# Expert weights in eighteen places instead of sixteen, token rows kept once in fp32 and gathered by fp32 products

## The reference

```python
def expert_choice_ffn(h, w_router, w_gate, w_up, w_down):   # h: 512 tokens x 1024
    cap = CAPACITY_FACTOR * seq // N_EXPERTS                 # 64 tokens for each of 16 experts
    aff = softmax(h @ w_router)
    gate, idx = lax.top_k(aff.transpose(0, 2, 1), cap)       # each expert chooses its tokens
    xe = h[idx]                                              # gather: 16 x 64 rows
    a = silu(xe @ w_gate) * (xe @ w_up)                      # 1024 x 1024 each
    ye = (a @ w_down) * gate
    y = zeros.at[idx].add(ye)                                # scatter
```

## Time and profile before

| | us |
|---|---|
| median of 3 runs | 1550.1 (1548.37 to 1550.99) |
| span of the profiled execution | 1550.0 |
| PE busy | 1457.8 (94%) |
| PEld busy | 955.4 (62%) |
| DVE busy | 615.2 (40%) |
| ACT busy | 492.6 (32%) |
| POOL busy | 74.5 (5%) |
| L809, the expert weights' products, busy | 351.1 |
| chain that ended last: PE | 76% |
| chain that ended last: DMA | 11% |
| of it DMA of `w_up`, `w_gate`, `w_down` | 5%, 4%, 2% |
| HBM read | 303.35 MB |

### The profile page before, as it was taken

How to read it: one execution, slowest core, us unless ns; L and a number is a source line. 1 busy time by engine, 2 the same in 40 slices (tenths; PEclk the granted TensorE clock), 3 DMA queues, 4 the chain that set the end, 5 groups by cost and what they waited for, 6 DMA issues and landing times.

```text
span 1550.0 us, 17611 instructions
## 1 busy us (share of the span) xinstructions
PE 1457.8 (94%) x7135; PEld 955.4 (62%) x7135; DVE 615.2 (40%) x1192; ACT 492.6 (32%) x912; POOL 74.5 (5%) x100
## 2 busy tenths in 40 slices
PE   8988988999999999999997999988898999999998
PEld 6855366455434433433323899966686888888886
DVE  5366666344122222222215532136675443154325
ACT  6355276331001101101104412367734333123321
POOL 2000000100000000000002200000001111001100
PEclk9999999998999999999998999999999999999999
DMA  7476350318999999999995131140011332233201
GB/s 231 81 291 266 127 246 1 149 62 343 421 421 421 421 422 420 422 421 421 421 421 210 42 108 56 56 163 1 31 65 55 109 109 88 76 109 109 105 32 55
DMA packets 82738, 310.27 MB, mean 200 GB/s; under 512 B 7188, under 2 KB 43309, under 8 KB 55906
## 3 DMA queue, kind: packets, MB, share of 16 engines
q1 hardware_dynamic: 80656, 305.34, 50.3%
q10 hardware_dynamic: 1202, 2.15, 1.2%
q0 software_dynamic: 800, 1.66, 0.4%
HBM read 303.35 MB, written 5.78 MB: 199 GB/s over the span
## 4 chain that ended last, share of the span: by engine, by line
PE 76%; DMA 11%; ACT 5%; DVE 5%; issue 1%; SPq 0%; DVEq 0%; ACTq 0%
PE ps L809 15%; PE ps L433 13%; PE ps L434 13%; PE ps L435 13%; DMA sb<-in_w_up 5%; PE ps L663 4%; DMA sb<-in_w_gate 4%; DMA sb<-in_w_down 2%; PE ps L760 1%; PE ps L530 1%; ACT sb L1072 1%; PE ps L936 1%; PE ps L797 1%; PE ps L574 1%; PE ps L620 1%
## 5 line engine op out<-in xcount | busy, mean ns | idle before, releaser
L809 PE MATMUL ps<-sb 128*64 128x512 f32 x1536 | 351.1, 598 | 12.6 <-DMA sb<-in_w_gate 4.3
L809 PEld LDWEIGHTS ps<-sb 128*64 128x64 f32 x1536 | 103.3, 136 | 217.4 <-issue 181.9
L1072 ACT ACTIVATE sb<-ps 128x512 f32<-128x512 f32 (+4 forms) x168 | 86.2, 528 | 251.0 <-PE ps L785 73.1
L434 PE MATMUL ps<-r_fl,r_top 128*128 128x512 f32 x344 | 135.1, 393 | 0.0
L435 PE MATMUL ps<-r_act,r_low 128*128 128x512 f32 x344 | 134.8, 392 | 0.0
L433 PE MATMUL ps<-r_act,r_top 128*128 128x512 f32 x344 | 134.3, 390 | 0.0
L2095 DVE TENSOR_TENSOR r_low<-raw,r_top 128x2048 fp32r<-128x2048 f32 x33 | 74.2, 2290 | 78.7 <-ACT r_top L1072 78.7
L1877 DVE TENSOR_TENSOR sb<-sb,ps 128x512 f32<-128x512 f32 x64 | 44.0, 688 | 140.9 <-PE ps L798 140.9
L1072 ACT ACTIVATE r_top<-raw 128x2048 fp32r<-128x2048 f32 x33 | 61.4, 1908 | 69.7 <-PE ps L435 69.7
L433 PE MATMUL ps<-r_low,r_h 128*128 128x256 f32 x288 | 82.4, 286 | 1.0 <-ACT sb L1072 1.0
L434 PE MATMUL ps<-r_low,r_h 128*128 128x256 f32 x288 | 82.2, 285 | 0.0
(11 more groups left out here) (397 smaller groups left out, 2438.1 us busy)
## 6 DMA issues: line engine op xcount, KB each, us to landing
sb<-in_w_up SPq DMA_DIRECT2D x64, 1024.0 KB, 26.0
sb<-in_w_gate SPq DMA_DIRECT2D x64, 1024.0 KB, 25.5
sb<-in_w_down SPq DMA_DIRECT2D x64, 1024.0 KB, 26.3
sb<-in_w_mod SPq DMA_DIRECT2D x16, 1536.0 KB, 9.3
raw<-in_f_w_up SPq DMA_DIRECT2D x22, 1024.0 KB, 7.6
raw<-in_a_w_in SPq DMA_DIRECT2D x12, 1024.0 KB, 5.9
raw<-in_f_w_down SPq DMA_DIRECT2D x5, 2048.0 KB, 7.8
raw<-in_w_in SPq DMA_DIRECT2D x3, 1440.0 KB, 17.1
```

What stands on the lines that cost most here:

```text
L434: pe.matmul(o, a_hi, b_lo, start=False, stop=False)
L809: mm = pe.matmul(PS[64 * hf:64 * hf + 64, b * HALF:(b + 1) * HALF], lhsT(k), ring[c % RINGN][:, kk, hf * HALF:(hf + 1) * HALF], start=(k = ...
L1072: return act_(o, i_, ACT.Identity, bias=bias, scale=scale)
```

## The change

- The ring has 18 places. The two new ones are `QKV` and `QKV + 2048`, where `h2hi` was. The places are numbered anew, so that each of the loads ahead of the experts still goes to the memory that is free at that point; the chunk numbers in SP's program change with them. Chunks 16 and 17 are issued after `pe_bT (7, 1)`, the last transposes that read `QKV` in latent attention.
- `h2hi` and `h2lo` are gone, with ACT's four copies and DVE's four subtractions. The gather multiplies the one-hot matrix, read as fp32, with `h2` itself: 8 fp32 products for 16 fp32r products.
- `keep_busy` issues two products ahead of the wait for `pos`, where there was one, and one more after the transposes of the positions.
- The first three projection loads wait for the last chunk in their places by the new numbers (`last_chunk`).

```diff
-RINGN = 16
+RINGN = 18
...
-        RING_AT = SLOT_AT[10:14] + [MODROW, QKV + 6144] + SLOT_AT[0:10]
+        RING_AT = SLOT_AT[10:14] + [MODROW, QKV + 6144] + [SLOT_AT[n] for n in (3, 4, 5, 8, 9, 7, 0, 1, 2, 6)] + [QKV, QKV + SLOT]
...
-        h2hi = [place(f"r_h2hi{t}", QKV + t * D, D, F32R) for t in range(NT)]
-        h2lo = [place(f"r_h2lo{t}", Z + t * D, D, F32R) for t in range(NT)]
...
-            keep_busy(x, 1)
+            keep_busy(x, 2)
             pe.wait_ge(*at("pos"))
...
             tr.then_inc(*inc("pe_posT"))
+            keep_busy(nb("warm", banks=7), 1)
...
-                        if i == 0:
-                            pe.wait_ge(*at("h2hi", t))
-                            pe.wait_ge(*at("h2lo", t))
-                        for part in (h2hi, h2lo):
-                            mm = pe.matmul(bank(6 + hf), onehot[:, t, :], part[t][:, hf * HALF:(hf + 1) * HALF],
-                                           start=(t == 0 and part is h2hi), stop=(t == NT - 1 and part is h2lo))
+                        mm = pe.matmul(bank(6 + hf), onehot[:, t, :].bitcast(F32), h2[:, t, hf * HALF:(hf + 1) * HALF],
+                                       start=(t == 0), stop=(t == NT - 1))
...
-                copy(h2hi[t][:, :], h2[:, t, :]).then_inc(*inc("h2hi", t))
...
-            def h2_rest(t):
-                eng.wait_ge(*at("pe_h2T", (t, 1)))
-                eng.wait_ge(*at("h2hi", t))
-                ve.tensor_tensor(h2lo[t][:, :], h2[:, t, :], h2hi[t][:, :].bitcast(F32), ALU.subtract).then_inc(*inc("h2lo", t))
...
-                        h2_rest(t - 1)
...
-            h2_rest(3)
...
+            def last_chunk(place_):
+                return max(c for c in range(NCHUNK) if RING_AT[c % RINGN] == place_)
...
-            for c in range(6, 10):
+            for c in (12, 13, 14, 6):
+                expert_load(c)
+            sp.wait_ge(*at("pe_bT", (BH - 1, 1)))
+            for c in (16, 17):
                 expert_load(c)
...
-            for c in (10, 11):
+            for c in (7, 8):
...
-            for c in (14, 15, 2, 3):
+            for c in (9, 10, 2, 3):
...
-            expert_load(13)
+            expert_load(11)
             sp.wait_ge(*at("vc_out"))
-            expert_load(12)
+            expert_load(15)
...
-                sp.wait_ge(*(at(*proj_end(n - 3)) if n >= 3 else at("x_used", NCHUNK - 10 + n)))
+                sp.wait_ge(*(at(*proj_end(n - 3)) if n >= 3 else at("x_used", last_chunk(RING + n * SLOT))))
```

More of the change, by code:

```diff
@@ L70 @@
     "act_latent": "qb_a kv_a kr_ready qh kh Be ptB oTb",
-    "act_router": "h2T_a h2hi lge affT",
+    "act_router": "h2T_a lge affT",
     "act_proj": "xn_a hT_h hcT_h phi wg_hi gexp gln kl kc v_a floor osig",
@@ L80 @@
     "dve_latent": "qb_d kv_d kr0 krr_t krr qkn qrr_t qk mc gcols sumG ql_b kl_b negB Brec Bp",
-    "dve_router": "x1 rs2h h2 h2T_d h2lo lgx lgm lgs lgr aff topk sel slots pos posT",
+    "dve_router": "x1 rs2h h2 h2T_d lgx lgm lgs lgr aff topk sel slots pos posT",
     "pool_proj": "wg0 g0 hT_l hcT_l",
```

## The result

The changed kernel takes 1558.0 us (median of 5 runs, 1556.3 to 1558.8) against 1551.0 of the kernel before (5 runs beside it, 1548.4 to 1553.0). The ratio is 1.0045, 95% interval 1.0033 to 1.0057: slower, by 7.0 us. The forecast was 1556.9 us, +6.8.

What follows compares the result with a forecast made beforehand. TensorE and DMAs were taken as close limits, the DMAs deciding from pair 5 on. Dearer gathers +21.7, first gather +1.5, vanished waits -16.4 sum to +6.8 us on the median 1550.1: 1556.9 us, range 1552.5 to 1560.5.

Steps and rivals of the forecast that it cites:

- Who is last: Expert stage: TensorE's path ends it at 834.4 us; the DMAs bring the last chunk 10 us too early.
- undisturbed TensorE 811.2: Expert stage before the change: TensorE alone would have ended it at 811.2 us, without 16.4 us of waits for DMAs.
- The stream: Expert weight loads: two chunks shorter, 5.0 us earlier, less 1.5 for a later start; last chunk lands at 822.2.
- The price of a gather: Gathers 1 to 7 in the expert stage: fp32 products cost 3.10 us more each, +21.7 us in all.
- The first gather: Gather ahead of the expert weights: 6.87 us at full clock for 5.36, so the stage starts 1.5 us later.
- The end of the stage: Expert stage on TensorE's own path: 811.2 + 21.7 + 1.5 = 834.4 us.
- After the stage: First three projection loads behind the last expert chunk: in time before and after, 0 us.
- The two loads: Chunks 16 and 17, issued after the transposes of 244.71 to 246.6 us while the DMAs are idle: 0 us.
- That the DMAs decide: Rival for the expert stage: it ends with the stream of loads, -3.5 us, 1546.6 us; chance 7%.
- PEld's low busy share: Sign for the faster rival: weight loads' row busy only 21.48 of 55.10 us, so TensorE would have headroom.
- The slow clock: Rival at the first gather: half clock adds 1.7 us, 1558.6, up to 1563.8 if all runs slow; chance 14%.
- The break-even of 2.1 us a gather: Gathers in the expert stage: outcome even if each grows by (16.4 - 1.5) / 7 = 2.1 us, against 3.1 expected.

Runs made afterwards that it cites:

- e1: Changed kernel with sixteen ring places again and early loads as before the change, fp32 gather kept: 1559.7 us, ratio 1.0069 to the kernel before.
- e5: The changed kernel itself, unaltered, run once more in another job: 1558.7 us, ratio 1.0052 to the kernel before.
- e2: Changed kernel, eighteen places, but gathering with 16 fp32r products of rows rounded once, each tile multiplied twice: 1546.0 us, ratio 0.9971 to the kernel before.
- e9: Changed kernel with each fp32 product of the gather issued twice: 1613.0 us, ratio 1.040 to the kernel before.
- e4: Changed kernel with `keep_busy` as before, one product ahead of the positions' transposes and none behind: 1558.7 us, ratio 1.0055 to the kernel before.
- e7: Kernel before without the gather's `h2lo` products, 8 fp32r products for 16: 1549.8 us, ratio 0.9999 to the kernel before.
- e10: Changed kernel, eighteen places, gathering with 8 fp32r products of rounded rows, one a tile: 1544.8 us, ratio 0.9961 to the kernel before.
- the bf16 version: Eighteen places, gather of 16 products on two bf16 row parts, added products kept: 1543.2 and 1546.5 us, ratios 0.9955 and 0.9970 to the kernel before.

## Why the prediction was right, point by point

**Who is last.** This carried the forecast, and it held: undisturbed TensorE 811.2 + gathers against the stream of loads. The waits that I put at 16.4 us are gone. The stage's length says so: it grew by 452.4 - 446.5 = 5.9 us, and seven gathers at +3.21 are 22.5; the difference, 16.6, is what was waited before.

**The stream** was to bring its last chunk at 822.2. The DMAs of the changed kernel moved 421 GB/s from 810 to 815 us, 403 to 820 and 317 to 825, with the projection loads in it from 798 on; that is about where it was put. e1 ends its stage at the same length with the stream two chunks longer, so its end was not what TensorE waited for.

**The price of a gather** was 3.10 by `w_o`'s products and is 58.40 - 55.19 = 3.21. The gather's 16 records take 6.97 us where `w_o`'s took 6.87. Right to 0.8 us in the sum.

**The first gather** was to cost +1.5 and cost 6.97 - 5.36 = 1.6, at full clock, as expected. Yet the first weights start only 0.94 us later, 381.39. The chain ahead of it began earlier: the last transposes of `h2` (L709, L711 before) took 1.29 us instead of 1.94, and DVE's copy of them started at 347.32 instead of 347.82:

```profile
346.66 1.29 PE L709 MATMUL ps<-sb 128*128 128x128 f32 x8 [1.55 <-DVE sb L1786]
347.32 0.69 DVE L1755 COPY sb<-ps 128x512 f32<-128x512 f32 x1
```

Both kernels idle there for 1.6 us; the granted clock from 347 to 349 us was 0.79 in this run and 0.50 in the one before. The removed copies have no part in it: top-k still begins on ACT's copy, at 355.70, 1.87 us of DVE's idle behind it (before, 0.73 with the subtraction in between).

**The end of the stage** was forecast for 834.4 and is at 834.43 (827.34 + 7.09): the gathers were put 0.8 too low and the start 0.6 too high, which nearly cancels. That the end is met to 0.1 us is luck of these two errors.

**After the stage** I had 0; the span grew by 5.9 where the stage's end moved by 6.8. The scatter of the last pair ran on the full clock in this run (one product every 0.23 us from 837.2 on), and before on the slow one for its first half (one every 0.43 us from 830.5 to 833.5). The transposes behind it begin 8.25 us after the stage's end, 8.81 before, so 0.56 of the 0.9 us are there; the rest I have not traced. It is small beside what this part does from trace to trace: from the start of the last weights' product to the end of the span it is 722.1 to 727.4 us in the thirteen traces, 722.1 and 725.7 in the two of the changed kernel. So the medians' +7.0 us meet the forecast's +6.8 more closely than they can be trusted: the profiled pair gives +5.9, and e5 gives +8.4 against the median of its own job. What the runs bear out is the stage's length.

**The two loads** were to be issued at 246.6; they went out at 253.32. I took the transposes of 244.71 for the last ones, but those of the last head are at 252.6. It costs nothing, since SP's next load waits until 278.55:

```profile
253.32 0.80 SPq L2259 DMA_DIRECT2D sb<-in_w_down  x2
278.55 0.38 SPq L2268 DMA_DIRECT2D sb<-in_x  x1
```

**The rivals.** That the DMAs decide, at -3.5 us, is what e2 measured with the cheap gather, and e9 shows that a product's price is paid in full. PEld's low busy share, on which that rival leaned, was no sign of slack: in the changed kernel it was 20.5 of 55 us while TensorE had no hole. By the rule of the Trainium skill (Perfetto Trace Analysis, § Identifying the Most-Contended Engine) this share would measure TensorE's headroom; here it does not. The slow clock did not come; e4 shows that without the added products it would have, at a price of 1.7 us. The break-even of 2.1 us a gather was not tried from close by: gathers of 1.9 us less and of 0 more lie on the flat side (e7, e10, e2), +3.2 and +10.1 on the steep one (the changed kernel, e9).

## What to carry to other kernels

Where two engines run side by side at nearly the same pace, write down both end times, the one of the stream and the one of the engine alone, before memory is traded for work: a deeper buffer lowers only the first, and a dearer step raises only the second. Here 16 us of waits stood between them. So by the sum the first 2.3 us that each of seven gathers grew were free (16.4 / 7), and the rest was paid; the runs show the two sides of this point and not the point itself. If a buffer needs the room of split operands, look for a narrower split that keeps single passes before going to full-width products, and weigh the bits it gives up.

## What the runs showed that I had not expected

- A bf16 product of 512 columns starts every 0.215 us, an fp32r one every 0.228 (464.51 to 468.28 for 16 gives 0.236 with the first), half an fp32 one every 0.43.
- The clock's falls shift from run to run. The first gather began at 368.06 us in e7 and at 372.27 us in the kernel before, though these two have the same program up to there. Of these 4.2 us, 3.6 are there at the first product of `w_o` (275.90 and 279.48). From 100 to 125 us the granted clock was 0.93 in e7 and 0.86 in the kernel before, from 125 to 150 us 1.00 and 0.93. That points to the clock; I have not traced the whole to it.
- Medians of one kernel move by 2 to 3 us between jobs. The stage's length was 452.4 us in all five traces with single fp32 gathers, on 16 and on 18 places, and 441.7 and 442.0 us in the two of the bf16 version. It told kernels apart where the times could not.
- A load that waits for something else can take from a stage what a shorter step ahead of it gives (e7, e10), since the stream stands behind it in the queue.
